# Two of four layer-norm blocks computed by GpSimd in place, and ten warming matmuls that start from a first memset

## The reference, cut to what matters

```
def _layernorm(x, g, b):
    mu = jnp.mean(xf, axis=-1, keepdims=True)
    xc = xf - mu
    y = xc * lax.rsqrt(jnp.mean(xc * xc, axis=-1, keepdims=True) + EPS)
    return y * g + b
def _sgu(u, v, ln_g, ln_b, w_s, b_s):
    v = _layernorm(jax.nn.gelu(v, approximate=False), ln_g, ln_b)
    mixed = jnp.einsum('gts,bnsgc->bntgc', tril(w_s), vc) + b_s
    return jax.nn.gelu(u, approximate=False) * mixed
```

## Time and profile before

| | us |
|---|---|
| median of three runs (lowest to highest) | 1646.99 (1646.91 to 1647.17) |
| the profiled execution | 1646.85 |
| its span, first to last instruction | 1645.1 |
| TensorE busy (matmuls) | 1637.0 |
| VectorE busy | 969.2 |
| ScalarE busy | 783.1 |
| GpSimd busy | 50.8 |

### The profile page before, as it was taken

The page is one execution under the profiler, slowest core; times in us unless marked ns, Lnnn a source line. Parts: engine busy times, 40 slices in busy tenths (PEclk is TensorE's granted clock), DMA queues, the critical chain, the costliest instruction groups (busy, mean ns, idle before and its releaser), DMA issues.

```text
span 1645.1 us, 20945 instructions
## 1 busy us (share of the span) xinstructions
PE 1637.0 (100%) x7394; PEld 1360.0 (83%) x7394; DVE 969.2 (59%) x1302; ACT 783.1 (48%) x1113; POOL 50.8 (3%) x49
## 2 busy tenths in 40 slices
PE   9999999999999999999999999999999999999999
PEld 7888888888888888888888888888888888888887
DVE  6898887554554434434648988875455444344344
ACT  7788886333343223223457788763334432232231
POOL 1000000000110000000120000000001100000000
PEclk9999999999999999999999999999999999999999
DMA  5222222223323233232332222223233232322323
GB/s 194 95 71 77 77 86 74 97 89 102 102 91 101 94 99 98 94 103 89 124 120 90 77 77 77 78 77 98 93 102 102 90 102 90 102 92 100 96 95 128
DMA packets 46860, 158.15 MB, mean 96 GB/s; under 512 B 5456, under 2 KB 5712, under 8 KB 46800
## 3 DMA queue, kind: packets, MB, share of 16 engines
q1 hardware_dynamic: 46656, 157.34, 29.1%
q10 hardware_dynamic: 144, 0.03, 0.0%
HBM read 155.26 MB, written 2.10 MB: 96 GB/s over the span
## 4 chain that ended last, share of the span: by engine, by line
PE 88%; DVE 7%; ACT 3%; DVEq 1%; ACTq 1%; issue 1%
PE bank L461 26%; PE bank L462 26%; PE bank L465 26%; PE z L489 2%; PE z L563 1%; PE bank L489 1%; PE z L461 1%; PE z L465 1%; PE z L462 1%; DVE w_lo L1179 1%; DVE s_lo L1212 1%; PE misc L586 0%; PE misc L583 0%; DVE t_s L1207 0%; PE z L552 0%
## 5 line engine op out<-in xcount | busy, mean ns | idle before, releaser
L461 PE MATMUL bank<-xg_hi,w_hi 128*128 128x512 f32 x1472 | 574.5, 390 | 0.0
L462 PE MATMUL bank<-xg_lo,w_hi 128*128 128x512 f32 x1472 | 573.4, 390 | 0.0
L789 ACT ACTIVATE w_hi<-raw 128x1024 fp32r<-128x1024 f32 (+1 forms) x294 | 302.2, 1033 | 472.6 <-DMA raw<-in_w_units 472.2
L1179 DVE TENSOR_TENSOR w_lo<-raw,w_hi 128x1024 fp32r<-128x1024 f32 (+1 forms) x294 | 357.1, 1218 | 39.4 <-ACT w_hi L789 22.4
L465 PE MATMUL bank<-xg_hi,w_lo 128*128 128x512 f32 x1472 | 364.1, 389 | 0.0
L465 PEld LDWEIGHTS bank<-xg_hi,w_lo 128*128 128x128 f32 x1472 | 276.2, 188 | 57.2
L462 PEld LDWEIGHTS bank<-xg_lo,w_hi 128*128 128x128 f32 x1472 | 276.5, 188 | 56.7
L461 PEld LDWEIGHTS bank<-xg_hi,w_hi 128*128 128x128 f32 x1472 | 276.4, 188 | 56.8
L1184 DVE TENSOR_TENSOR S<-bank,rstd 128x512 f32<-128x512 f32 x152 | 104.9, 690 | 255.2 <-PE bank L465 253.6
L461 PE MATMUL bank<-mid_hi,w_hi 128*128 128x512 f32 x474 | 184.7, 390 | 0.0
L462 PE MATMUL bank<-mid_lo,w_hi 128*128 128x512 f32 x474 | 184.4, 389 | 0.0
(11 more groups left out here) (204 smaller groups left out, 1708.9 us busy)
## 6 DMA issues: line engine op xcount, KB each, us to landing
raw<-in_w_units SPq DMA_DIRECT2D x278, 512.0 KB, 3.3
raw<-in_w_units SPq DMA_DIRECT2D x20, 256.0 KB, 2.6
xT<-in_x SPq DMA_DIRECT2D x8, 256.0 KB, 6.6
out_x<-xT SPq DMA_DIRECT2D x7, 256.0 KB, 4.0
ln_g<-in_sgu_ln_g SPq DMA_DIRECT2D x2, 256.0 KB, 5.0
ln_b<-in_sgu_ln_b SPq DMA_DIRECT2D x2, 256.0 KB, 5.2
sgu_bias<-in_sgu_b SPq DMA_DIRECT2D x2, 256.0 KB, 5.7
sw_raw<-in_sgu_w SPq DMA_DIRECT2D x2, 256.0 KB, 5.8
```

The costliest lines, as they stand in the source:

```text
L461: mm(dst[:, :], wh[:, k0 + k, :], his[k], start=(k % per == 0), stop=False)
L462: mm(dst[:, :], wh[:, k0 + k, :], los[k], start=False, stop=False)
L789: af(w_hi[at.slot(c)][:, 0:kc, :], raw[at.slot(c)][:, 0:kc, :], ACT.Copy).then_inc(hi_done, 1)
L1179: tt(w[:, 0:kc, :], r[:, 0:kc, :], h[:, 0:kc, :].bitcast(F32), ALU.subtract).then_inc(lo_done, 1)
```

## The change

Blocks 2 and 3 leave VectorE. GpSimd computes them in `v_tok` itself (`late_norm`), with three instructions each, as soon as VectorE has told that `ln_rstd` is there. ScalarE rounds both in one place, ahead of the first `fold_halves`, and VectorE subtracts both in one place, after `square_lo` in `pair(0)`. At the start the memset stands ahead of the ten increments, and ten matmuls run in place of eight.

```
-WARM = 8
+WARM = 10
...
+        def ln_block(n):
+            return (S0[:, :], S1[:, :], v_tok[:, 2, :], v_tok[:, 3, :])[n].rearrange("p (g c) -> p g c", g=KC)
...
+            def late_norm(n):
+
+                e = v_tok[:, n, :]
+                nc.gpsimd.tensor_scalar(e, e, ln_mv[:, n, 0:1], ln_rstd[:, n:n + 1], ALU.subtract, ALU.mult)
+                pool.drain()
+                nc.gpsimd.tensor_tensor(e, e, ln_g[:, :], ALU.mult)
+                pool.drain()
+                nc.gpsimd.tensor_tensor(e, e, ln_b[:, :], ALU.add).then_inc(ln_late, 1)
+                pool.drain()
...
+                pool.wait_ge(ln_in, l * 48 + 48)
+                pool.wait_ge(ln_scaled, l + 1)
+                for n in (2, 3):
+                    late_norm(n)
                 for half in range(2 if l + 1 < L else 1):
                     add_squares(l * 2 + half)
...
-                act.wait_ge(ln_pre, l * NT + n + 1)
-                af(yb_hi[:, :, n * P:(n + 1) * P], (S0, S1)[n % 2][:, :].rearrange("p (g c) -> p g c", g=KC),
-                   ACT.Copy).then_inc(ln_hi, 1)
+                if n < 2:
+                    act.wait_ge(ln_pre, l * 2 + n + 1)
+                else:
+                    act.wait_ge(ln_late, l * 2 + n - 1)
+                af(yb_hi[:, :, n * P:(n + 1) * P], ln_block(n), ACT.Copy).then_inc(ln_hi, 1)
...
-                    if j == 0:
-                        ln_round(l, 2)
...
-                    if j == 0:
-                        ln_round(l, 3)
...
                 softplus_logs(l * 24)
+                ln_round(l, 2)
+                ln_round(l, 3)
                 fold_halves(l * 24)
...
+            nc.vector.memset(N0[:, 0:P], -1.0).then_inc(warm_in, 1)
             dve.sem_inc(unit_done, RAW)
...
-            nc.vector.memset(N0[:, 0:P], -1.0).then_inc(warm_in, 1)
...
                 stt(ln_rstd[:, :], ln_t[:, :], 1.5, ln_r[:, :], ALU.add, ALU.mult)
                 dve.drain()
+                dve.sem_inc(ln_scaled, 1)
...
                         scaled(at, 0, gates[:, KC, :])
-                        layer_norm(2)
                         square_lo(l * 8 + 2)
+                        layer_norm_lo(2)
+                        layer_norm_lo(3)
...
                     attention_lo(h3)
-                    if j == 0:
-                        layer_norm_lo(2)
...
                     causal(h3 + 3)
-                    if j == 0:
-                        layer_norm(3)
...
                     yc_add(heads, 0)
-                    if j == 0:
-                        layer_norm_lo(3)
```

More of the change, by code:

```diff
@@ L255, in build @@
         ln_chain = sem("ln_chain")
+        ln_scaled = sem("ln_scaled")
         ln_pre = sem("ln_pre")
+        ln_late = sem("ln_late")
         ln_hi = sem("ln_hi")
@@ L1341, in layer_norm @@
                 def layer_norm(n):
-                    e = (S0, S1)[n % 2]
-                    if n >= 2:
-                        dve.drain()
+                    e = (S0, S1)[n]
                     stt(e[:, :], v_tok[:, n, :], ln_mv[:, n, 0:1], ln_g[:, :], ALU.subtract, ALU.mult)
@@ L1351, in layer_norm_lo @@
                     dve.wait_ge(ln_hi, l * 4 + n + 1)
-                    tt(yb_lo[:, :, n * P:(n + 1) * P], (S0, S1)[n % 2][:, :].rearrange("p (g c) -> p g c", g=KC),
+                    tt(yb_lo[:, :, n * P:(n + 1) * P], ln_block(n),
                        yb_hi[:, :, n * P:(n + 1) * P].bitcast(F32), ALU.subtract).then_inc(ln_ok, 1)
```

## The result

The change makes the kernel slower: 1653.16 us median of 7 runs (1651.18 to 1653.63) against 1647.12 (1646.86 to 1647.80) of the kernel before, a ratio of 1.0033 with a 95% interval from 1.0023 to 1.0044. The forecast was 1651.0, slower, with a range from 1646.0 to 1655.5. The seven times lie in two groups: two at 1651.2, with a mean granted clock of 0.999, and five at 1653.1 to 1653.6, with 0.997. The profiled execution is of the second group, at 1653.09.

The account below looks back on a forecast made before the run. TensorE was taken to bound the kernel, busy 1637.0 of 1645.1 us. From 1646.85, two layers at 2.1 late added 4.2 and the start took 0.15; with the median 0.14 above, 1651.0 (range 1646.0 to 1655.5).

Parts of the forecast that it names:

- The two waits: TensorE waits at `cumulate` for `fold_hl`, 1.69 us, and at `mix` for VectorE's block 3 subtraction, 0.35: 2.04 a layer.
- What is removed: Without blocks 2 and 3 on VectorE, its chain to `fold_hl` comes 2.9 us earlier: 1.96, 0.34 and 0.59.
- What is added: From about 53 us, GpSimd's six instructions take turns with seven two-input VectorE instructions, each waiting for the other's whole instruction.
- The delay D: How much later VectorE finishes k because of the turns with GpSimd: 5.0 us, between 4.6 and 6.0.
- the term of the tensor_scalar: Time of GpSimd's tensor_scalar within the turns up to k: 0.65 us taken, bounds 0.47 and 1.15.
- the sign that I had named for being wrong: VectorE's rows at 53 to 58 us keep their 0.75, or k is late and the scores start on time.
- The stall at the scores: TensorE's scores wait for `k_rest` and begin at 66.13 in place of 62.33: a new stall of 3.8 us a layer.
- Where the two meet again: At `cumulate` of head 3, TensorE is ready at 137.85 and VectorE at 138.1, so VectorE decides; 2.1 us late a layer.
- The start: Earlier memset and ten warming matmuls speed TensorE's first real matmuls: -0.15 us, bounds -0.15 and +0.1.
- the clock: Rival: TensorE's clock falls in the scores' pause, 2 us a layer lost, 1655; shared chance 0.10 with a long tensor_scalar.
- the first: Rival: the turns cost VectorE next to nothing as GpSimd always gives way, both old waits go, 1642.7; chance 0.16.
- the second: Rival: fewer turns, k near 3 us late, scores stall 1.7, delay and gain cancel, 1647.0; chance 0.16.

Follow-up runs that it names:

- e4_relief_only: The change without GpSimd's six instructions in each layer, so blocks 2 and 3 are not normalised: 1642.38 us, ratio 0.9969 to the kernel before.
- e6_tt_only: The change with GpSimd's four tensor_tensors alone in each layer, its tensor_scalars left out: 1650.39 us, ratio 1.0017 to the kernel before.
- e3_late_start: The change with GpSimd released behind `k_rest` and ScalarE's two roundings behind `fold_round`: 1642.67 us, ratio 0.9972 to the kernel before.
- e2_filled: The change with 26 spare matmuls ahead of each layer's first scores, keeping TensorE busy: 1650.37 us, ratio 1.0019 to the kernel before.
- e8_cost_only: The kernel before with the change's start and GpSimd's six instructions writing to a spare tile, VectorE still doing all blocks: 1656.77 us, ratio 1.0054.
- e5_ts_only: The change with GpSimd's two tensor_scalars alone in each layer, its tensor_tensors left out: 1643.25 us, ratio 0.9973 to the kernel before.

## Why the prediction was right, point by point

**What bounds the kernel**: right. The two waits were nearly all there was to win. `e4_relief_only` wins 4.7 us in the span, where they and the start were sized at 4.2; side by side with the trace before, the change has 0.45 and 1.78 less at the two places, 2.2 a layer for 2.04.

**What is removed**: right. 2.9 us of VectorE's chain were forecast; `fold_hl` begins at 132.21 in `e4_relief_only` for 134.89, 2.7.

**What is added**: the mechanism is right for four of the six instructions. Two-input instructions of VectorE and tensor_tensors of GpSimd take turns, and `e6_tt_only` shows it alone. The Trainium skill's rule ("SBUF — State Buffer", "Who interferes with whom") agrees with that. It does not with the tensor_scalars: these read SBUF too, last 2.3 to 3.0 us, and VectorE lost 0.32 to 0.35 to each, or nothing (`e3_late_start`); the measurement decides.

**The delay D**: 5.0 was forecast (4.6 to 6.0) at k, with nothing added behind it. Measured are 2.7 at k and 1.76 more at `k_rest`, 4.46 where the scores wait for it; that this is near 5.0 is luck. Two errors offset each other, both from the term of the tensor_scalar, which was mis-sized twice: it takes 2.61 and 2.31 us, beyond the 1.15 that I gave as its upper bound, and costs VectorE a third of a us, below the 0.47 that I gave as its lower one. The one moved GpSimd's end from 62.2 to 64.7, onto `k_rest`, which I had as free (1.76); the other spared the norms of blocks 0 and 1. So the sign that I had named for being wrong came in part: of VectorE's rows from 53 to 58 us, those at 54.60 and 55.42 kept their 0.74 and 0.75, the one at 53.58 lost a third of a us, and only those at 56.09 and 57.95 took turns.

**The stall at the scores**: 3.8 forecast, 3.30 measured, where it was forecast, behind VectorE's late `k_both`.

**Where the two meet again**: VectorE, 2.1 late, was to decide at `cumulate` of head 3 by 0.25. With the clock up (`e2_filled`) it is 1.36 late and decides by 0.15. In the change itself TensorE decides, as it is later still.

**The start**: -0.15 forecast, -0.24 in the change's profile; by the other profiles with the same start neither is told from nothing.

**The sum** was +4.0, and is +6.0. The time lies just inside the forecast's own range (to 1653.2), but that end stood for a D of 6.0, which did not come: with the clock up (`e2_filled`) the loss is 2.9 us, or 3.3 in the span. The term that is missing is the clock. It stood among the rivals, with 0.10 and with 2 us a layer; it came, with 3.0 us in all by `e2_filled`. The step that failed is the inference from the pause of 1.69 us: that pause left no slow stretch, and I gave a pause of 3.8 us a chance of only 0.10 to leave one. It was 3.13 us, and stretches of 3.4 and 6.8 us at 0.5 followed. The other rivals fall as forecasts of the time, by `e6_tt_only` and `e8_cost_only`: the tensor_tensors' turns are paid in full. But each had a part of the mechanism. For the two tensor_scalars the first holds: `e5_ts_only` runs at 1643.25, near its 1642.7. And there were fewer turns up to k, where the 2.7 is near the second's D of 3; what that rival lacked is `k_rest`. The Trainium skill's rule that the idle array falls back to half its clock ("TensorE: Matmul & The Clock Gate", Part 1) agrees with the rows at 0.5.

## What to carry to other kernels

Before work is handed to GpSimd, lay its stretch beside VectorE's rows and ask of each whether both its inputs are tiles in SBUF: here it was those that took turns with GpSimd's two-input instructions, and these cost nothing only where VectorE read PSUM or waited. Release such work by the step after the next hand-over that TensorE waits for, not by the moment its data are ready, and put whoever consumes it where it is ready by then: here those two moves turned +6.0 us into -4.8. Price a new stall of some 3 us on TensorE with the slower clock behind it; here 26 spare matmuls in each pause kept the clock up.

## What was not expected of the hardware

A tensor_scalar on GpSimd with two numbers for each partition, 128x512, takes 2.31 to 3.00 us; a tensor_tensor of the same size 1.29 where it waits for nothing (64.76 in `e3_late_start`). The one that reads fewer tiles is the slower.

While it ran, VectorE's two-input instructions were delayed once at most: in the change and in `e5_ts_only` one beside each tensor_scalar, by a third of a us, and in `e3_late_start` none. What makes the difference was not tested.

TensorE's clock fell behind some pauses and not behind others of the same length, in one execution even (2.6 us, `e6_tt_only`), and for different times (3.4 and 6.8 us behind 3.13, in the change). In the runs without a trace only the mean clock is on record: 0.999 of some 1650 us is an estimated 3.3 us at half clock, and 0.997 is 9.9, which fits the change's two groups of times. What decides it in a run stays open.
